# One phase for the final norm, the modulation and the norm rows; turning and splitting inside the projection

## The chip, the cores and the metric

The program runs on one core of one Trainium2 chip. It is one launch; the metric is the device time of that launch in microseconds, from the first to the last instruction and what lies around them. The core has a matrix engine (TensorE, PE in the profile, its weight loads PEld), three elementwise engines (VectorE or DVE, ScalarE or ACT, GpSimd or POOL), a SyncE queue (SP) that only issues transfers here, and 16 DMA engines. Everything is float32; large products are made from operands split into two float32r parts (hi and lo, three products each).

## What is computed

Two layers of a first block, its final norm, and then a second block that takes the normed rows as `x`. The part around the change, cut from the reference:

```python
x = rms_norm(x, final_g)                              # end of the first block, x: 512 x 1024
mod_x = jnp.split(jax.nn.silu(c) @ w_mod + b_mod, 6)  # second block; w_mod: 1024 x 6144
mod_c = ...                                           # the same for c_ctx
zx = modulate(rmsnorm(x, norm1_g), mod_x[0], mod_x[1]) @ w_in
zc = modulate(rmsnorm(ctx, norm1_g), mod_c[0], mod_c[1]) @ w_in   # ctx: 256 x 1024
...
x = x + mod_x[2] * merge_branches(...)
x = x + mod_x[5] * peer_ffn(modulate(rmsnorm(x, norm2_g), mod_x[3], mod_x[4]), ...)
```

`modulate(h, shift, scale)` is `h * (1 + scale) + shift`. So of the six 1024-wide parts of the modulation, four (0, 1, 3, 4) are needed as columns (one number per channel) and two (2, 5), the gates, as rows spread over all partitions.

## The kernel before

The kernel is a chain of phases. Each `Phase` allocates semaphores, opens a block in which every engine has its own list of instructions, and ends with a barrier of all engines. Within an engine the list runs in the order written; between engines only semaphores set the order. Rows of tokens lie in tiles of 128 (`ST` = 4 for x, `CT` = 2 for the context, `AT` = 6 for both), the 1024 channels in `DC` = 8 chunks of 128.

Between the last product of the first block and the first one of the second, these phases run one after the other:

- `load_phase` for `final_g` (`fg`), then `norm_phase` with `write_back`: ScalarE sums the squares of four row tiles, VectorE scales each tile in place (L213).
- `modulation_phases`: a `load_phase` of six small transfers, a phase for the silu (`csil`) and a copy of it spread 128 wide (`cwide`), then `plain_gemm_phase` over the twelve blocks of `w_mod` (each 1024 x 512, 2048 KB, ring `wbuf_mod` of four, loaded by SyncE at L356). For eight blocks TensorE multiplies `csil` (2 columns) by the block, eight chunks into one bank of `psum` (L367), and VectorE copies two rows out (L1251). For the four gate blocks it multiplies `cwide`, so that the sum comes out on all 128 partitions, and VectorE adds the bias rows (L1258). A last phase turns the pairs into columns with small products (L1274) and VectorE makes `affine` from them.
- `load_phase` of the context rows, then `norm_phase` through `modulated_norm` twice, for 2 and for 4 tiles: squares, root, scaled rows (L210), transposes (L226), modulation out of `psum` into `hT_whole` (L1299).
- `split_phase`: ScalarE writes `hT_all.hi` (L578), VectorE `hT_all.lo` (L584), SyncE spills `x` and `hT_whole` to HBM (L563) and loads the rope tables and gains (L569).
- `gemm_phase`, the projection: six blocks of `w_in_2`, each loaded in four quarters of 512 KB through `w_raw` (a ring of 2 here), cast to hi by ScalarE (L521), lo by VectorE (L534), and multiplied (L472). A quarter's lo frees its place in the ring. `HeadNorm` is its side: an object whose methods are called at given places of each engine's list; `lead_vector` builds tables before the first quarter, and later it norms and rotates rows of q and k while the next groups are multiplied. In the fifth and sixth block, groups of transposes (`Turns`, L458) stand between the groups of products.

A second `gemm_phase`, in the last stage of the kernel, already has a norm as its side: `ModulatedLead` makes norm rows, transposes them ahead of the first product, and modulates and splits two chunks between every two weight quarters (L318, L312, L322). A third one, after the attention, has `MixerSpill` as its side, whose transfers are issued by GpSimd while the first weights load.

## Time and profile before

| | |
|---|---|
| median of 3 runs | 5360.02 us (5355.99 to 5365.32) |
| profiled execution | 5353.26 us, span 5351.4 us |
| TensorE busy | 4554.2 us, 85% of the span |
| VectorE busy | 3130.4 us, 58% |
| ScalarE, GpSimd busy | 1602.2 us, 739.5 us |
| mean granted TensorE clock | 0.933 of full speed |

The page also cuts the span into 40 equal slices of 134 us and gives each engine's busy share in tenths. TensorE stands at 7 to 9 in nearly all of them; slices 13 and 14 (1605 to 1873 us), in which the phases listed above lie, are both at 7. The share is an average over stages that have little to do with each other, so a question on one stage is put to the timeline of that stage: the instructions of each engine in order of time, with the idle time before each and what ended it. Times there are microseconds from the start of the span.

### The profile page before, as it was taken

Reading aid. Unit: us, or ns where it says so; the run is one execution under the profiler, and the core shown is the slowest. Engines: PE = TensorE matmul, PEld = TensorE weight load, DVE = VectorE, ACT = ScalarE, POOL = GpSimd, SP = SyncE. Lnnn points to the kernel's source line nnn. Section 1 sums busy time; section 2 is a strip of 40 time slices with the busy share of each in tenths; the row PEclk is TensorE's granted clock in tenths of the full one; section 3 lists DMA queues with packets and bytes.
Section 4 is the critical chain, followed back from the end, with each engine's and each line's share of the span. In section 5 each row is a group of like instructions: output and inputs, shape, how many; then the busy total and the mean of one; then the engine's idle time right before and its main releaser. Section 6 shows DMA issues by size and latency. Waiting matters only on the chain. (4 is left out here: it accounts for less than half of the span.)

```text
span 5351.4 us, 57195 instructions
## 1 busy us (share of the span) xinstructions
PE 4554.2 (85%) x20624; PEld 3197.2 (60%) x20624; DVE 3130.4 (58%) x6299; ACT 1602.2 (30%) x3154; POOL 739.5 (14%) x650
## 2 busy tenths in 40 slices
PE   7878998978997597788999999997986877777777
PEld 5636886735884285566888888886862333333333
DVE  5563224563221265755777777753438888888886
ACT  3233342233341133312544444543221111111111
POOL 0000010000110000010000000000004444444443
PEclk9978998978998799988999999998998999999998
DMA  3002332101334320041000000004229999999998
GB/s 117 32 0 79 102 98 75 48 1 63 100 98 159 128 75 2 1 151 63 10 12 12 12 12 12 12 3 142 89 71 382 419 412 416 414 410 413 410 413 346
DMA packets 142504, 777.72 MB, mean 145 GB/s; under 512 B 18932, under 2 KB 23924, under 8 KB 74120
## 3 DMA queue, kind: packets, MB, share of 16 engines
q0 software_dynamic: 78576, 557.79, 25.5%
q1 hardware_dynamic: 63640, 216.19, 12.1%
q8 instruction: 169, 2.77, 0.2%
q14 instruction: 119, 0.97, 0.1%
HBM read 753.99 MB, written 19.92 MB: 145 GB/s over the span
## 5 line engine op out<-in xcount | busy, mean ns | idle before, releaser
L2730 PE MATMUL psum<-rows,diag 128*128 128x512 f32 x2048 | 999.0, 645 | 317.7 <-ACT diag L2709 313.2
L2730 PEld LDWEIGHTS psum<-rows,diag 128*128 128x128 f32 x2048 | 411.1, 206 | 887.8 <-issue 887.8
L534 DVE TENSOR_TENSOR w_split_lo<-w_raw,w_split_hi 128x1024 fp32r<-128x1024 f32 (+1 forms) x316 | 379.4, 1209 | 649.2 <-ACT w_split_hi L521 644.4
L2620 POOL DMA_INDIRECT rows<-in_peer_uv,sel_idx x512 | 614.9, 1201 | 935.4 <-PE psum L2730 648.3
L2635 DVE SCALAR_TENSOR_TENSOR uh<-rows,h_rows 128x1024 f32<-128x1024 f32 x512 | 627.8, 1226 | 181.6 <-DMA rows<-in_peer_uv,sel_idx 153.3
L521 ACT CAST w_split_hi<-w_raw 128x1024 fp32r<-128x1024 f32 (+1 forms) x316 | 322.8, 1028 | 788.5 <-PE psum L472 465.7
L2702 ACT ACTIVATE g<-g 128x4 f32<-128x4 f32 x128 | 26.3, 205 | 1077.0 <-DVE g L2646 1077.0
L740 POOL TENSOR_TENSOR uT_lo<-normed_rows,uT_hi 128x512 fp32r<-128x512 f32 x64 | 82.8, 1294 | 1378.9 <-ACT uT_hi L716 1378.9
L1812 PE MATMUL psum<-X_wide,wAT_wide 128*128 128x128 f32 x1920 | 262.2, 280 | 1.1 <-DVE X_wide L2156 1.1
L1812 PEld LDWEIGHTS psum<-X_wide,wAT_wide 128*128 128x128 f32 x1920 | 234.8, 192 | 34.3 <-issue 31.2
L1823 PE MATMUL psum<-U_wide,Y_wide 128*128 128x128 f32 x1536 | 206.0, 277 | 0.0
L472 PE MATMUL psum<-hT_mlp_hi,w_split_hi 128*128 128x512 f32 x512 | 199.6, 390 | 2.2 <-DVE hT_mlp_lo L287 2.2
L1823 PEld LDWEIGHTS psum<-U_wide,Y_wide 128*128 128x128 f32 x1536 | 188.0, 192 | 19.0 <-issue 18.7
L472 PE MATMUL psum<-hT_mlp_hi,w_split_lo 128*128 128x512 f32 x512 | 199.2, 389 | 0.0
L472 PE MATMUL psum<-hT_mlp_lo,w_split_hi 128*128 128x512 f32 x512 | 199.2, 389 | 0.0
L472 PE MATMUL psum<-w_split_hi,uT_hi 128*128 128x512 f32 x512 | 199.2, 389 | 0.0
L472 PE MATMUL psum<-w_split_lo,uT_hi 128*128 128x512 f32 x512 | 199.2, 389 | 0.0
L472 PE MATMUL psum<-w_split_hi,uT_lo 128*128 128x512 f32 x512 | 199.2, 389 | 0.0
L1993 ACT COPY U_wide<-psum 128x512 f32<-128x512 f32 x240 | 140.6, 586 | 187.5 <-PE psum L1812 184.0
L2124 DVE SCALAR_TENSOR_TENSOR wS<-psum,pl,wP 128x128 f32<-128x128 f32 x160 | 54.8, 343 | 204.7 <-PE psum L1888 204.7
L2709 ACT ACTIVATE diag<-ident_sb,g 128x128 f32<-128x128 f32 x512 | 163.5, 390 | 36.6 <-DVE g L2651 36.6
L2353 POOL DMA_DIRECT2D merge_stage<-hT_spill x8 | 4.3, 538 | 1178.9 <-POOLq L168 1170.9
(471 smaller groups left out, 9299.7 us busy)
## 6 DMA issues: line engine op xcount, KB each, us to landing
w_raw<-in_w_in SPq DMA_DIRECT2D x120, 512.0 KB, 4.7
w_raw<-in_w_up SPq DMA_DIRECT2D x64, 512.0 KB, 4.3
w_raw<-in_w_down SPq DMA_DIRECT2D x64, 512.0 KB, 4.4
wbuf_mod<-in_w_mod SPq DMA_DIRECT2D x12, 2048.0 KB, 7.5
w_raw<-in_w_out SPq DMA_DIRECT2D x24, 512.0 KB, 5.1
w_raw<-in_peer_wq SPq DMA_DIRECT2D x16, 512.0 KB, 4.8
rows<-in_peer_uv,sel_idx POOLq DMA_INDIRECT x512, 13.2
w_raw<-in_w_branch_a SPq DMA_DIRECT2D x8, 512.0 KB, 4.5
```

The costliest lines, as they stand in the source:

```text
L472: last = nc.tensor.matmul(psum[0:rows, bank, 0:cols], l_, r_, start=(start and c == 0 and j == 0), stop=(stop and c == len(pairs) - 1 and ...
L521: nc.scalar.copy(ring.hi[:, q % SPLIT_RING, :, 0:w], raw[:, q % raw_ring, :, 0:w]).then_inc(hi_ready, 1)
L534: nc.vector.tensor_tensor(ring.lo[:, q % SPLIT_RING, :, 0:w], raw[:, q % raw_ring, :, 0:w], ring.hi[:, q % SPLIT_RING, :, 0:w].bitcast(F32 ...
L740: return nc.gpsimd.tensor_tensor(uT.lo[:, k, :], squares[:, k % 2, :], uT.hi[:, k, :].bitcast(F32), ALU.subtract)
L1812: last = nc.tensor.matmul(psum[:, b, i * P:(i + 1) * P], flat(wAT[:, c]), flat(X[:, c]), start=True, stop=True)
L1823: last = nc.tensor.matmul(psum[:, b, i * P:(i + 1) * P], l_, r_, start=True, stop=True)
L1993: nc.scalar.copy(flat4(U[:, batch(b)]), psum[:, b, :]).then_inc(u_copied, 1)
L2124: nc.vector.scalar_tensor_tensor(wS[:], psum[:, 5, 0:P], scale, wP[:], ALU.mult, ALU.add).then_inc(s_copied, 1)
L2620: nc.gpsimd.indirect_dma_start(out=rows[:, n % RB, :], out_offset=None, in_=I["peer_uv"], in_offset=bass.IndirectOffsetOnAxis(ap=sel[:, t, ...
L2635: nc.vector.scalar_tensor_tensor(prod[:], rows[:, n % RB, 0:D], 1.0, h[:, t, :], ALU.mult, ALU.mult, accum_out=dots[:, (n // BATCH) % 2, s ...
L2709: nc.scalar.activation(diag[:, n % (2 * BATCH), :], ident[:], ACT.Copy, scale=g2[:, b % 2, i:i + 1]).then_inc(diag_ready, 1)
L2730: last = nc.tensor.matmul(psum[:, 2 * (t % 2) + half, :], diag[:, n % (2 * BATCH), :], rows[:, n % RB, D + half * NB:D + (half + 1) * NB], ...
```

## The change

All phases before the projection become one, `modulation_phase`. In it:

- SyncE loads the condition vector and then the twelve blocks of `w_mod` in another order (pairs and gates in turn); the other small loads, the context rows and `final_g` are issued by GpSimd.
- ScalarE and VectorE make the final norm and, after it, the norm rows of context and x (`xn`, in what will be `v`), between the pieces of the modulation.
- The gates leave TensorE: VectorE multiplies and adds the eight chunks of a gate block with the silu as a scalar per partition (`sum_gate`), and TensorE spreads the sum over the partitions with one product by ones (`spread`).
- The columns are turned in two halves (`columns`).

The projection gets `ModulatedHeads` as its side, which adds to `HeadNorm` what `norm_phase` and `split_phase` did: transposes ahead of the first product, modulation and split of two chunks after each weight quarter, the context's transposes as four `Turns` in the first block, spills and table loads from GpSimd. The tables are built in the second block.

```diff
+def modulation_phase(nc, T, x, xn, sb):
...
+    BLOCKS = ((0, 0), (0, 1), (1, 0), (1, 1), (2, 0), (3, 0), (2, 1), (3, 1), (5, 0), (4, 0), (5, 1), (4, 1))
...
+        @block.sync
+        def _(sp):
+            sp.dma_start(csil[:], I["c"]).then_inc(cond_loaded, 16)
+            for b, (m, half) in enumerate(BLOCKS):
+                before = b - SLOTS4
+                if before in pairs:
+                    sp.wait_ge(pair_ready, pairs.index(before) + 1)
+                elif before in gates:
+                    sp.wait_ge(gate_summed, gates.index(before) + 1)
+                sp.dma_start(wbuf[:, b % SLOTS4], I["w_mod"][2 * m + half]).then_inc(block_loaded[b % SLOTS4], 16)
...
+            def sum_gate(i):
...
+                chain.after(nc.vector.tensor_scalar(a, wbuf[:, b % SLOTS4, 0, :], csil[:, 0, 0:1], None, ALU.mult))
+                for c in range(1, DC):
+                    ins = nc.vector.scalar_tensor_tensor(a, wbuf[:, b % SLOTS4, c, :], csil[:, c, 0:1], a, ALU.mult,
+                                                         ALU.add)
...
+            for i in range(4):
+                pair(i)
+            columns(0)
+            pair(4)
+            spread(0)
+            pair(5)
+            spread(1)
+            pair(6)
+            spread(2)
+            pair(7)
+            spread(3)
+            columns(1)
...
+class ModulatedHeads(HeadNorm):
...
+    def gpsimd(self, pool):
+        nc = self.nc
+        nc.gpsimd.dma_start(*self.x_to).then_inc(self.x_spilled, 16)
+        pool.wait_ge(self.x_spilled, 16)
+        for dst, src in self.table_loads:
+            nc.gpsimd.dma_start(dst, src).then_inc(self.tables_loaded, 16)
+        for c in range(DC):
+            pool.wait_ge(self.whole_ready, c + 1)
+            nc.gpsimd.dma_start(self.hT_to[:, c, :], self.whole[:, c, CTX:]).then_inc(self.hT_spilled, 16)
...
+    def quarter_scalar(self, act, chain, q):
+        for c in range(QC * q, QC * q + QC):
+            act.wait_ge(self.whole_ready, c + 1)
+            self.nc.scalar.copy(self.hT.hi[:, c, CTX:], self.whole[:, c, CTX:]).then_inc(self.hi_scaled, 1)
+
+    def quarter_vector(self, dve, chain, q):
+        for c in range(QC * q, QC * q + QC):
+            dve.wait_ge(self.transposed, c + 1)
+            self.modulate(self.whole[:, c, CTX:], self.psum[:, c, :], 0, c).then_inc(self.whole_ready, 1)
+        for c in range(QC * q, QC * q + QC):
+            dve.wait_ge(self.hi_scaled, c + 1)
+            self.nc.vector.tensor_tensor(self.hT.lo[:, c, CTX:], self.whole[:, c, CTX:],
+                                         self.hT.hi[:, c, CTX:].bitcast(F32), ALU.subtract
+                                         ).then_inc(self.operand_ready, 1)
+
+    def operand(self, pe, b, c):
+        if b == 0:
+            pe.wait_ge(self.operand_ready, c + 1)
+        if b == 2 and c == 0:
+            pe.wait_ge(self.ctx_ready, 4)
...
+        if (b, g) == (1, 3):
+            act.wait_ge(self.hT_spilled, 16 * DC)
+            act.wait_ge(self.ctx_ready, 4)
...
+        if (b, g) == (1, 1):
+            dve.wait_ge(self.tables_loaded, 16 * len(self.table_loads))
+            self.tables(dve)
+        if (b, g) == (1, 3):
+            dve.wait_ge(self.hT_spilled, 16 * DC)
```

TensorE's list from the modulation to the first product of the projection: before, with `wbuf_mod` the blocks, `cwide` and `csil` the silu, `nscr` the norm rows:

```order
L367 MATMUL psum<-wbuf_mod,csil 2x512 x32
L367 MATMUL psum<-wbuf_mod,cwide 128x512 x16
L367 MATMUL psum<-wbuf_mod,csil 2x512 x32
L367 MATMUL psum<-wbuf_mod,cwide 128x512 x16
...
L1274 MATMUL psum<-ident_sb,mod_rows 128x2 x32
...
L226 MATMUL psum<-ident_sb,nscr 128x128 x16
...
L226 MATMUL psum<-ident_sb,nscr 128x128 x32
```

The same stretch of TensorE's list now, in which the last row stands in the projection's own phase and `arena` holds the norm rows:

```order
L1253 MATMUL psum<-wbuf_mod,csil 2x512 x32
L1271 MATMUL psum<-ident_sb,mod_rows 128x2 x16
L1253 MATMUL psum<-wbuf_mod,csil 2x512 x8
L1263 MATMUL psum<-gate_sums,ones_all 128x512
...
L1253 MATMUL psum<-wbuf_mod,csil 2x512 x8
L1263 MATMUL psum<-gate_sums,ones_all 128x512
L1271 MATMUL psum<-ident_sb,mod_rows 128x2 x16
...
L1425 MATMUL psum<-ident_sb,arena 128x128 x32
```

The 32 products by `cwide` are gone and four by ones stand between the last four pairs; the small products are in two halves, one of them in the middle.

VectorE's list before, from the final norm (L213) through the modulation to the first norm rows (`nscr`) and `hT_whole`:

```order
L213 SCALAR_TENSOR_TENSOR x<-x,stats,fg 128x1024 x4
...
L1251 COPY mod_rows<-psum 2x512 x4
L1258 TENSOR_TENSOR gate_rows<-psum,gate_rows 128x512 x2
L1251 COPY mod_rows<-psum 2x512 x4
L1258 TENSOR_TENSOR gate_rows<-psum,gate_rows 128x512 x2
...
L210 TENSOR_SCALAR nscr<-x,stats 128x1024 x4
L1299 TENSOR_SCALAR hT_whole<-psum,affine 128x512 x8
```

VectorE's list now, from the final norm to the first gate sum, and then the start of the projection:

```order
L1165 SCALAR_TENSOR_TENSOR x<-x,final_stats,fg 128x1024 x4
L1182 COPY mod_rows<-psum 2x512
L1170 TENSOR_SCALAR norm_stats<-norm_stats 128x6
L1173 RECIPROCAL norm_stats<-norm_stats 128x6
...
L1182 COPY mod_rows<-psum 2x512
L1193 TENSOR_SCALAR gate_sums<-wbuf_mod,csil 128x512
L1195 SCALAR_TENSOR_TENSOR gate_sums<-wbuf_mod,csil,gate_sums 128x512 x7
L1182 COPY mod_rows<-psum 2x512 x2
...
L419 TENSOR_TENSOR w_split9_lo<-w_raw9,w_split9_hi 128x1024
L1430 TENSOR_SCALAR arena<-psum,affine 128x512 x2
L1444 TENSOR_TENSOR hT_all_lo<-arena,hT_all_hi 128x512 x2
```

The norm work stands among the copies of the pairs, each gate sum takes eight instructions, and the modulation and the split of x stand behind each weight quarter.

GpSimd's list, empty in this stretch before, now starts the projection with the spill of `x`, on which its table loads wait:

```order
L1414 DMA x_spill<-x 128x4096
L1417 DMA x<-in_ropeC 128x384
L1417 DMA x<-in_ropeS 128x384
L1417 DMA x<-in_q_gain 128x128
L1417 DMA x<-in_k_gain 128x128
L1420 DMA hT_spill<-arena 128x512 x8
```

Six transfers that SyncE issued ahead of the projection are now thirteen of GpSimd's during it.

## Rows read from the trace of the kernel before

**Rows 1.** Stages: us; busy (instructions) of PE, PEld, DVE, ACT, POOL; clock; DMA share; GB/s
```profile
1666.40:1863.70 197.30, 108.23 (x305) 42.50 (x305) 40.92 (x68) 23.55 (x39) 0.00 (x0) 0.74 0.44 171
1879.00:2045.00 166.00, 166.00 (x772) 138.24 (x771) 95.47 (x114) 48.89 (x70) 0.00 (x0) 1.00 0.17 55
```

**Rows 2.** SyncE's timeline: start, us, engine, line, operation, out<-in, count
```profile
1667.40 0.35 SPq L178 DMA_DIRECT2D fg<-in_final_g  x1
...
1694.55 68.12 SPq L356 DMA_DIRECT2D wbuf_mod<-in_w_mod  x12
1806.57 0.33 SPq L178 DMA_DIRECT2D ctx_rows<-in_ctx  x1
...
1857.34 94.95 SPq L441 DMA_DIRECT2D w_raw<-in_w_in  x20
```

**Rows 3.** TensorE's timeline, modulation, small products, first and fourth quarter of the projection
```profile
1701.94 9.89 PE L367 MATMUL psum<-wbuf_mod,csil 128*2 128x512 f32 x16 [36.24 <-DMA wbuf_mod<-in_w_mod]
1711.98 7.03 PE L367 MATMUL psum<-wbuf_mod,csil 128*2 128x512 f32 x16
1719.16 7.03 PE L367 MATMUL psum<-wbuf_mod,csil 128*2 128x512 f32 x16
...
1784.60 7.11 PE L367 MATMUL psum<-wbuf_mod,cwide 128*128 128x512 f32 x16 [0.30 <-PE psum L367]
1793.22 10.81 PE L1274 MATMUL psum<-ident_sb,mod_rows 2*128 2x2 f32 x64 [1.51 <-PEq L168]
...
1871.94 0.50 PE L472 MATMUL psum<-w_split_hi,hT_all_hi 128*128 128x512 f32 x1 [0.41 <-DVE w_split_lo L534]
```

**Rows 4.** Stages as in Rows 1: first weights landing; the small products
```profile
1702.00:1709.00 7.00, 7.00 (x10) 1.04 (x11) 0.00 (x0) 0.00 (x0) 0.00 (x0) 0.59 0.99 424
...
1791.70:1795.00 3.30, 1.79 (x18) 1.81 (x17) 0.69 (x1) 0.00 (x0) 0.00 (x0) 1.00 0.02 5
1795.00:1798.00 3.00, 3.00 (x23) 3.00 (x22) 0.00 (x0) 0.00 (x0) 0.00 (x0) 0.75 0.00 0
```

**Rows 5.** VectorE's groups: line, operation, out<-in, count | busy, mean ns | idle before
```profile
L815 DVE SCALAR_TENSOR_TENSOR av<-qkpad,taps,av 128x512 f32<-128x512 f32 x64 | 48.1, 752 | 2.3
L813 DVE TENSOR_SCALAR av<-qkpad,taps 128x512 f32<-128x512 f32 x16 | 7.6, 477 | 0.0
L1251 DVE COPY mod_rows<-psum 2x512 f32<-2x512 f32 x8 | 5.4, 679 | 63.8 <-PE psum L367 63.8
```

**Rows 6.** VectorE's timeline at the end of the modulation
```profile
1804.06 0.42 DVE L1286 TENSOR_TENSOR modc<-psum,bcol 128x32 f32<-128x32 f32 x2 [11.63 <-PE psum L1274]
...
1805.53 0.17 DVE L1291 COPY affine<-modc 128x8 f32<-128x8 f32 x1
```

**Rows 7.** Timelines of ScalarE and TensorE: first weight quarter of the projection; the phase with `ModulatedLead`
```profile
1861.33 1.04 ACT L521 CAST w_split_hi<-w_raw 128x1024 fp32r<-128x1024 f32 x1 [14.78 <-DMA w_raw<-in_w_in]
...
3896.33 1.03 ACT L521 CAST w_split_hi<-w_raw 128x1024 fp32r<-128x1024 f32 x1
...
3913.92 0.47 PE L472 MATMUL psum<-hT_ps_hi,w_split_hi 128*128 128x512 f32 x1 [1.40 <-DVE hT_ps_lo L322]
```

**Rows 8.** VectorE and ScalarE: third weight quarter, projection and the phase with `MixerSpill`
```profile
1862.41 2.46 DVE L534 TENSOR_TENSOR w_split_lo<-w_raw,w_split_hi 128x1024 fp32r<-128x1024 f32 x2 [3.06 <-ACT w_split_hi L521]
1867.52 1.05 ACT L521 CAST w_split_hi<-w_raw 128x1024 fp32r<-128x1024 f32 x1 [3.91 <-DMA w_raw<-in_w_in]
...
2291.15 2.52 DVE L534 TENSOR_TENSOR w_split_lo<-w_raw,w_split_hi 128x1024 fp32r<-128x1024 f32 x2 [10.85 <-ACT w_split_hi L521]
2300.95 1.04 ACT L521 CAST w_split_hi<-w_raw 128x1024 fp32r<-128x1024 f32 x1 [8.53 <-DMA w_raw<-in_w_in]
```

**Rows 9.** TensorE's timeline in the fifth block; GpSimd's timeline in the last projection
```profile
1982.24 1.04 PE L458 MATMUL psum<-ident_sb,q_rows 128*128 128x128 f32 x8
1983.03 0.47 PE L472 MATMUL psum<-w_split_hi,hT_all_hi 128*128 128x512 f32 x1
...
3656.76 2.13 POOL L2353 DMA_DIRECT2D merge_stage<-hT_spill  x4 [1170.93 <-POOLq L168]
```

More of the change, by code:

```diff
@@ L551, in _ @@
                         tail(n).then_inc(tail_done, 1)
-def split_phase(nc, src, dst, spill=None, source=None, also=()):
-    with Phase(nc, ["hi_ready", "spilled", "moved"] + [f"chunk_loaded{c}" for c in range(DC)]) as (
-            block, hi_ready, spilled, moved, *chunk_loaded):
-        @block.sync
-        def _(sp):
-            if spill is not None:
-                for to, what in spill:
-                    sp.dma_start(to, what).then_inc(spilled, 16)
-                sp.wait_ge(spilled, 16 * len(spill))
-            if source is not None:
-                for c in range(DC):
-                    sp.dma_start(src[:, c, :], source[:, c, :]).then_inc(chunk_loaded[c], 16)
-            for d_, s_ in also:
-                sp.dma_start(d_, s_).then_inc(moved, 16)
-            if also:
-                sp.wait_ge(moved, 16 * len(also))
-        @block.scalar
-        def _(act):
-            for c in range(DC):
-                if source is not None:
-                    act.wait_ge(chunk_loaded[c], 16)
-                nc.scalar.copy(dst.hi[:, c, :], src[:, c, :]).then_inc(hi_ready, 1)
-        @block.vector
-        def _(dve):
-            for c in range(DC):
-                dve.wait_ge(hi_ready, c + 1)
-                nc.vector.tensor_tensor(dst.lo[:, c, :], src[:, c, :], dst.hi[:, c, :].bitcast(F32), ALU.subtract)
 def hybrid_layer(nc, l, T):
@@ L1272, in _ @@
                     for c in range(DC):
                         at = 2 * (q * DC + c)
-                        last = nc.tensor.matmul(psum[:, 0, at:at + 2], mod_rows[:, q, c * P:(c + 1) * P],
-                                                T["ident"][0:2, 0:2], start=True, stop=True)
+                        last = nc.tensor.matmul(psum[:, 6 + h, at:at + 2], rows[:, 2 * h + q, c * P:(c + 1) * P],
+                                                ident[0:2, 0:2], start=True, stop=True)
                 last.then_inc(columns_ready, 1)
-            @block.vector
@@ L1336, in turned, with tables @@
         return src[:, t, half * NB:(half + 1) * NB]
-    def lead_vector(self, dve, chain):
+    def tables(self, dve):
         nc = self.nc
@@ L2804, in sba, with with_context, both @@
                 return att.enter_context(nc.sbuf_tensor(name, shape, dt))
-            share = Share(arena)
-            v, k = share.take([AT, D]), share.take([AT, D])
             q = sba("q_rows", [P, ST, D])
             with nc.sbuf_tensor("head_squares", [P, D], F32) as sq:
-                heads = HeadNorm(nc, T, q, k, room, sq, (ropes, gains))
+                whole = k.rearrange("p t n -> p (t n)").rearrange("p (c n) -> p c n", c=DC)
+                heads = ModulatedHeads(nc, T, q, k, room, sq, (ropes, gains), v, whole, hT, (x_d, x[:]), hT_d,
+                                       [(ropes[:, 0], I["ropeC"]), (ropes[:, 1], I["ropeS"]),
+                                        (gains[:, 0], I["q_gain"].to_broadcast([P, 2, 64])),
+                                        (gains[:, 1], I["k_gain"].to_broadcast([P, 2, 64]))])
+                def with_context(groups):
+                    def both(w):
+                        g = groups(w)
+                        r = [heads.ctx_turns(j) for j in range(4)]
+                        return [g[0], r[0], g[1], r[1], g[2], r[2], r[3], g[3]]
+                    return both
                 def with_turns(groups, order):
```

387 lines of the change are left out of this document (210 added, 177 removed).

## Prediction

> **What bounds the kernel now.** I began with the engines' busy shares and the 40 slices: TensorE leads, but an average says nothing of one stage. So I put the question to the stage that the change rewrites. From VectorE's last addition of the first block to the first product of the projection 197.3 us pass [rows 1]. In them TensorE is busy 108.2 us, VectorE 40.9, ScalarE 23.6 and the DMA engines 44% of the time: nothing is full. SyncE's timeline shows why. It is a row of starts, each behind a barrier: the final gain at 1667.4, the first modulation block at 1694.6, the context rows at 1806.6, the projection's weights at 1857.3 [rows 2]. The path that sets the end runs through all of it, since nothing else is in flight.
>
> Two stretches of it are work at a limit. The modulation's twelve blocks occupy TensorE from 1701.94 to 1784.60 + 7.11 = 1791.7, at 7.18 us a block once the clock is up (7.03 busy, the next starts 1719.16 − 1711.98 = 7.18 later); the first takes 9.89 because it begins at the lower clock [rows 3]. The mean granted clock of 1702 to 1709 is 0.59 of 2.4 GHz [rows 4]. The rest, some 107 us, is loads, norms, barriers and splits with TensorE mostly idle.
>
> Behind it, from 1879 to 2045, the projection keeps TensorE busy for all of 166.0 us at the full clock, with VectorE busy 95.5 us of them and ScalarE 48.9 [rows 1]. So what this stage gains arrives at the end of the kernel, unless the projection gives it back, and every TensorE instruction added to the projection is paid in full.
>
> **The new modulation phase, step by step.** Times continue the trace's own clock. I follow TensorE's list, since it is the longest one, and look at the others as cover.
>
> Start. SyncE's first issue stands at 1667.4 as before; the condition vector takes 0.4 us of its queue, so block 0 is issued at 1667.8. Before, issue to first product took 1701.94 − 1694.55 = 7.4 us [rows 2, 3], alone on the engines. Now GpSimd's loads run beside it. The final gain spread over 128 partitions is 0.52 MB, 1.2 us at the 424 GB/s that the first blocks reached [rows 4]. First product: 1667.8 + 7.4 + 1.2 = **1676.4**. With no sharing it is 1675.2; with the 1.05 MB of context also ahead it is 1678.9. The silu needs only the condition vector and stands behind two square sums on ScalarE, so it is ready while block 0 is still landing.
>
> Four pairs: 9.89 + 0.15 + 3 × 7.18 = 31.6, to 1708.0. VectorE's copy 0.7 [rows 5], then the first half of the small products. Before, 64 records took 10.8 us [rows 3], but not evenly: 18 − 1 + 23 = 40 had begun by 1798, 4.8 us after their start, and between 1795 and 1798 the mean clock was 0.75, after 1.0 until 1795 [rows 4]: it had fallen to its lower level. So 32 of them take about 4.0 us, to **1712.7**, and leave TensorE at the lower clock: small products let it fall. The next pair then costs as much as a first one, 9.89 instead of 7.03, or 2.9 more. It would cost nothing if the clock held through only 32 records; I keep it, since they end in the stretch with 0.75.
>
> Four pairs and three products by ones: 4 × 7.18 + 2.9 + 3 × 0.9 (a block's 16 records take 7.03, so one product is two records, 0.88) = 34.3, to 1747.0. The last product by ones 0.9 beside VectorE's copy, the second half of the small products 4.0, VectorE's last step 0.8 (half of the sequence from 1804.06 to 1805.70) [rows 6]: 1752.7. From VectorE's last instruction to SyncE's next issue 1806.57 − 1805.70 = 0.9 passed [rows 2, 6]. The projection's first load is issued at **1753.6**, not at 1857.3.
>
> Cover for this: the transfers. Twelve blocks are 25.2 MB, GpSimd's loads 2.6; at 424 GB/s that is 66 us, under the 76 that TensorE's list takes. But the ring of four ties loads to uses. Block 9 goes into the place of block 5, whose pair is ready at 1722.8, and lands some 7.4 later, at 1730.2, when TensorE is done with the pair before it at 1730.9 plus a product by ones: just hidden. Block 11 queues behind 9 and 10 and lands at about 1740, where TensorE arrives at 1740.0. These two have no slack; each us of delay there costs one.
>
> Cover by VectorE: a gate sum is 0.48 + 7 × 0.79 = 6.0 us (0.75 an instruction and a wait between them) [rows 5], four of them 24 us. The first needs block 4 (landed by 1702) and must be over when TensorE wants the copies of pairs 2 and 3, at 1708. By this sum it is over at 1708. Late blocks push it beyond, up to 4 us. The final norm and the norm rows, a handful of long instructions, lie in the waits for pairs 0 and 1, which leave VectorE nearly 30 us.
>
> **The lead of the projection.** It now has the shape of `ModulatedLead`. There, from the cast of the first quarter at 3896.33 to the first product of the fourth quarter at 3913.92, after which TensorE does not stop, 17.6 us pass [rows 7]. The first quarter's cast comes 1861.33 − 1857.34 = 4.0 us after the load's issue [rows 2, 7]. What differs is the spill of x, 2.1 MB on GpSimd's queue at the same moment. No row has just this. The nearest is the phase with `MixerSpill`: there the third quarter was cast 2300.95 − 2293.67 = 7.3 us after VectorE freed both places, against 1867.52 − 1864.87 = 2.7 in the quiet case, so 4.6 us of delay beside 3.6 MB of GpSimd's transfers [rows 8]. Bounds 0 and 4.6; I take 2.0, less than half, since here the spill is smaller and only the first quarter has no slack (each later one has about 2 us). Fourth quarter: 1753.6 + 4.0 + 2.0 + 17.6 = **1777.2**, where before it was 1871.94 [rows 3]. That is 94.7 us earlier.
>
> A rule of the Trainium skill ("DMA: Bandwidth & Descriptors", the section on SWDGE, HWDGE and iDMA) bears on the 2.0: an engine takes turns between the queues of the two kinds. If a weight packet waits for one of four times its size each time, the whole spill goes ahead of the first quarter, and the estimate by that would be near 5 us (2.1 MB at the measured 424 GB/s), a time of 5270. The delay in the rows on `MixerSpill` agrees in kind; no row here shows the turns themselves.
>
> **What the projection pays.** The context's 16 transposes: eight took 0.79 us at the full clock [rows 9], so 1.6. VectorE gains some 10 us of modulation, split and tables in the first two blocks, where it had room; TensorE has all eight banks ahead of it and no new wait before block 2. The waits for the spill stand at the last group of block 1, about 40 us after the lead.
>
> **Sum.** 94.7 − 1.6 = 93.1 us. The profiled execution took 5353.3 us; minus 93.1 it is 5260.2. The median of the runs is 6.8 us above the profiled one; the forecast is made against the median: 5360.0 − 93.1 = **5266.9**.
>
> **Rivals.**
> *The lead starves.* The weights get little of the engines beside the spill, and a second quarter loses its slack too: the whole 4.6 at the first, 4 more at the third as in [rows 8]. For it: a ring of 2, and 16 KB of a partition in a row in the spill. Against: SyncE issues first and GpSimd's issue itself takes 0.53 [rows 9]. Price 6 to 7: 5273.
> *The ring binds the modulation.* Blocks 8 to 11 are freed by gate sums and pairs in turn; if the first sum ends late (DMA shared with GpSimd's loads) or the clock falls again in a gap, a 2.9 for each fall and up to 4 for the sum, the phase ends 7 to 10 later: 5276.
> *Less than thought.* The clock holds through the small products (2.9 back), no contention in the lead (2.0), none at the start (1.2): 5261.
> *Slower than before.* The spill holds the projection. ScalarE and VectorE both stop at the last group of block 1 until all eight pieces of `hT_spill` have landed, behind them the splits of block 2's weights, behind those TensorE. The pieces are due by about 1822 (1777 plus seven groups of 5.5 and the transposes). GpSimd has 13 issues from 1754 on, 0.53 each when nothing holds it [rows 9], 7 us in all, done by 1785. It decides from 5 us an issue on, and to lose 93 us more than 12 us an issue would be needed (13 × 12.4 = 161 us after 1754): above 5371. Nothing in the trace is near it.
> On this the Trainium skill has a rule that speaks against the change ("SBUF — State Buffer", the box on DVE blocking DMA): a transfer issued by GpSimd is held while VectorE copies in its fast mode, with 620 ns becoming 3100 ns. By that page 13 issues would take 40 us, ending at 1794, and nothing would be late. The trace has 0.53 an issue with VectorE at work in the same stage.
>
> **How the numbers follow.** Forecast (5262 to 5271) 0.50; lead starves 0.14; ring binds 0.20; less than thought 0.13; slower than before 0.01; 0.02 for a gain under 0.2%, if the gain is given back by something I don't see. About 0.2%, 11 us, is what a measurement can tell from no change. The terms' own ends, −6 and +13, with the runs' spread of −4 and +5, not all at once, give **5256 to 5284**, which also holds the first three rivals. Faster by over 0.2%: 0.97, same 0.02, slower 0.01.
>
> **What would show it.** The first pair near 1676 at the lower clock, its last near 1747; the clock at 0.5 after the first small products; SyncE's first projection weights near 1754; TensorE without a gap from about 1777; no idle time of TensorE in blocks 0 to 3. I am wrong if TensorE waits for VectorE's gate sums or for blocks 9 and 11, if the first quarter's cast comes more than 8 us after its issue, or if a later stage changes its length.

## The result and the profile after

The changed kernel took 5263.32 us (median of 4 runs, 5259.79 to 5289.91), the kernel before beside it 5358.86 us (4 runs, 5355.99 to 5365.32). The ratio is 0.9827, with a 95% interval of 0.981 to 0.9844: faster by 95.5 us. The forecast was 5266.9 us in a range of 5256 to 5284.

The profiled execution took 5262.22 us. Engines over the whole span, from its page:

```profile
span 5260.4 us, 56898 instructions
PE 4544.4 (86%) x20568; PEld 3189.7 (61%) x20568; DVE 3151.8 (60%) x6333; ACT 1603.0 (30%) x3153; POOL 753.5 (14%) x671
```

TensorE's work has fallen by 9.8 us only; the other 81 of the 91 us between the two spans are waits. SyncE's timeline (start, us, engine, line, operation, out<-in, count) has one start where [rows 2] have four:

```profile
1666.09 0.35 SPq L1107 DMA_DIRECT2D csil<-in_c  x1
1666.49 63.60 SPq L1114 DMA_DIRECT2D wbuf_mod<-in_w_mod  x12
1752.52 138.10 SPq L326 DMA_DIRECT2D w_raw<-in_w_in  x24
1958.38 0.33 SPq L178 DMA_DIRECT2D lam_rows<-in_diff_lambda  x1
```

The phase begins at 1666.09, where `fg` was issued at 1667.40 before [rows 2], so 1.3 us are scatter of what lies ahead. I count from this first issue. The projection's weights are issued 86.4 us after it (before 189.9), and `lam_rows`, the first load after the projection, 292.3 us after it. Before, `lam_rows` was issued at 2052.90, 385.5 us after the start. The stage has become **93.2 us** shorter; the sum said 93.1. Of the kernel before there is one traced execution only, so its 385.5 us carry the scatter of one.

TensorE's timeline, with the idle time before in brackets, is to be read beside [rows 3]:

```profile
1674.97 29.65 PE L1253 MATMUL psum<-wbuf_mod,csil 128*2 128x512 f32 x64 [10.59 <-DMA wbuf_mod<-in_w_mod]
1707.74 5.14 PE L1271 MATMUL psum<-ident_sb,mod_rows 2*128 2x2 f32 x32 [3.12 <-DVE mod_rows L1182]
1712.81 8.91 PE L1253 MATMUL psum<-wbuf_mod,csil 128*2 128x512 f32 x16
1721.65 1.13 PE L1263 MATMUL psum<-gate_sums,ones_all 128*128 128x512 f32 x2
...
1739.19 7.03 PE L1253 MATMUL psum<-wbuf_mod,csil 128*2 128x512 f32 x16 [0.38 <-DMA wbuf_mod<-in_w_mod]
1746.14 1.12 PE L1263 MATMUL psum<-gate_sums,ones_all 128*128 128x512 f32 x2
1747.20 3.77 PE L1271 MATMUL psum<-ident_sb,mod_rows 2*128 2x2 f32 x32
...
1775.77 0.47 PE L357 MATMUL psum<-w_split_hi,hT_all_hi 128*128 128x512 f32 x1 [1.41 <-DVE hT_all_lo L1444]
```

Two waits are worth reading. The 3.12 us ahead of the first small products are VectorE's: its timeline shows the copies of pairs 2 and 3 behind the whole first gate sum, although the products of both pairs were over by 1704.6.

```profile
1678.44 4.87 DVE L1165 SCALAR_TENSOR_TENSOR x<-x,final_stats,fg 128x1024 f32<-128x1024 f32 x4 [6.93 <-DMA fg<-in_final_g]
...
1700.50 0.49 DVE L1193 TENSOR_SCALAR gate_sums<-wbuf_mod,csil 128x512 f32<-128x512 f32 x1 [5.07 <-DMA wbuf_mod<-in_w_mod]
1701.03 5.48 DVE L1195 SCALAR_TENSOR_TENSOR gate_sums<-wbuf_mod,csil,gate_sums 128x512 f32<-128x512 f32 x7
1706.42 1.27 DVE L1182 COPY mod_rows<-psum 2x512 f32<-2x512 f32 x2
```

The other is in the projection's lead. Its first weight quarter is cast 4.85 us after its issue, and the third waits 0.85 us for its load (ScalarE's timeline):

```profile
1757.37 1.05 ACT L406 CAST w_split_hi<-w_raw 128x1024 fp32r<-128x1024 f32 x1 [61.38 <-DMA w_raw<-in_w_in]
...
1766.92 1.04 ACT L406 CAST w_split_hi<-w_raw 128x1024 fp32r<-128x1024 f32 x1 [0.85 <-DMA w_raw<-in_w_in]
```

while GpSimd's queue moves the spill of x, whose 2.1 MB take 13 us:

```profile
1752.99 0.54 POOL L1414 DMA_DIRECT2D x_spill<-x  x1 [82.23 <-POOLq L168]
1766.57 0.55 POOL L1417 DMA_DIRECT2D x<-in_ropeC  x1 [13.04 <-DMA x_spill<-x]
```

Stretches (us; busy of PE, PEld, DVE, ACT, POOL; clock; DMA share; GB/s): the projection as in the second of [rows 1], and the small products with the pair behind them, as in [rows 4]:

```profile
1780.00:1946.00 166.00, 166.00 (x772) 138.17 (x771) 104.23 (x130) 51.52 (x74) 0.00 (x0) 1.00 0.18 57
1707.00:1710.00 3.00, 2.26 (x20) 2.26 (x20) 0.69 (x2) 0.00 (x0) 0.00 (x0) 0.97 1.02 437
1710.00:1713.00 3.00, 3.00 (x15) 2.88 (x16) 0.08 (x1) 0.00 (x0) 0.00 (x0) 0.50 1.01 431
1713.00:1720.00 7.00, 7.00 (x13) 1.19 (x12) 6.34 (x13) 0.00 (x0) 0.00 (x0) 0.74 0.82 346
```

The projection has taken in VectorE's extra work (104.2 us busy where it had 95.5) and still holds TensorE busy for all of the 166 us.

All of TensorE's waits between the phase's start and the end of the projection fit in four rows (waited for: us in total, times, longest):

```profile
PE psum L1253 <- DMA wbuf_mod<-in_w_mod: 11.0, 2, 10.6
PE psum L357 <- DVE hT_all_lo L1444: 8.4, 4, 3.2
PE psum L1271 <- DVE mod_rows L1182: 3.1, 1, 3.1
PE psum L1425 <- PEq L168: 1.6, 1, 1.6
```

### The profile page after: what moved, and what is told of

It reads as the page before. It is cut to its first block and busy times, and to the rows that moved or that the text cites. A ratio compares the mean times of both kernels' runs of the same rounds, so it can differ in the third digit from the quotient of the medians.

```text
span 5260.4 us, 56898 instructions
## 1 busy us (share of the span) xinstructions
PE 4544.4 (86%) x20568; PEld 3189.7 (61%) x20568; DVE 3151.8 (60%) x6333; ACT 1603.0 (30%) x3153; POOL 753.5 (14%) x671
## 5 line engine op out<-in xcount | busy, mean ns | idle before, releaser
L2809 PE MATMUL psum<-rows,diag 128*128 128x512 f32 x2048 | 1019.7, 656 | 296.5 <-ACT diag L2788 295.1
L2714 DVE SCALAR_TENSOR_TENSOR uh<-rows,h_rows 128x1024 f32<-128x1024 f32 x512 | 628.0, 1227 | 181.0 <-DMA rows<-in_peer_uv,sel_idx 152.0
```

The source lines that it names most:

```text
L2714: nc.vector.scalar_tensor_tensor(prod[:], rows[:, n % RB, 0:D], 1.0, h[:, t, :], ALU.mult, ALU.mult, accum_out=dots[:, (n // BATCH) % 2, s ...
L2809: last = nc.tensor.matmul(psum[:, 2 * (t % 2) + half, :], diag[:, n % (2 * BATCH), :], rows[:, n % RB, D + half * NB:D + (half + 1) * NB], ...
```

## The experiments

A run's median moves by some microseconds, more than most of the terms in question. So each kernel has two readings: its time, and from its trace the distance from the phase's first issue to the first product of the projection's fourth quarter (Q4) and to the load of `lam_rows`. The last column, from there to the end of the span, is code whose work no experiment changes (the kernels with weights loaded ahead give a later phase's weight ring another place).

| | time, us (runs) | to Q4 | to `lam_rows` | rest |
|---|---|---|---|---|
| before | 5357.7 to 5363.1 (its medians beside the rows below) | 204.5 | 385.5 | 3298.5 |
| changed kernel | 5263.3 (4) | 109.7 | 292.3 | 3302.0 |
| the same again | 5264.0 (4) | 109.8 | 292.4 | 3302.2 |
| the same again | 5265.3 (5) | 109.1 | 291.7 | 3301.2 |
| modulation phase alone | 5287.4 (4) | 131.8 | 312.5 | 3304.7 |
| projection's part alone | 5339.3 (10) | 183.6 | 367.8 | 3321.9 |
| gates on TensorE | 5286.7 (4) | 129.1 | 313.2 | 3298.1 |
| first columns late | 5270.3 (4) | 113.1 | 295.7 | 3302.1 |
| first gate sum later | 5266.8 (4) | 107.9 | 292.4 | 3299.2 |
| spill of x later | 5263.8 (4) | 107.9 | 292.1 | 3303.0 |
| two quarters ahead | 5261.3 (4) | 105.4 | 289.5 | 3301.7 |
| two of the three | 5261.4 (5) | 104.0 | 288.2 | 3306.2 |
| all three | 5273.8 (5) | 103.0 | 285.6 | 3319.1 |
| all three again | 5259.4 (5) | 102.4 | 286.4 | 3308.1 |

**The changed kernel again**, to see how far two measurements of it differ.

> The changed kernel once more, as the reference for the others of its call. Both theories: 5263 us, a ratio of 0.982 to the kernel before, the first product of the projection's fourth weight quarter about 109.7 us after SyncE's first issue of the modulation phase.

5263.95 us, ratio 0.9816 (0.9785 to 0.9846). The wait ahead of the small products was there again, 3.24 us, so it is no accident of one execution.

**Each part alone.** First the merged phase, with turning, split and tables in phases of their own ahead of the projection:

```diff
+        turn_phase(nc, T, v, CT, 0, 1, whole, 0)
+        turn_phase(nc, T, v, ST, CT, 0, whole, CTX)
+        split_phase(nc, whole, hT, spill=[(x_d, x[:]), (hT_d, whole[:, :, CTX:])], also=[...])
...
-                heads = ModulatedHeads(nc, T, q, k, room, sq, ...)
+                heads = TableHeads(nc, T, q, k, room, sq, (ropes, gains))
...
-                gemm_phase(nc, psum, [(W[0], with_context(rows_of(q, 0, CT, ST))), ...
+                gemm_phase(nc, psum, [(W[0], rows_of(q, 0, CT, ST)), ...
```

> One part alone: the merged modulation phase stays, but the turning, the modulation, the split and the spills stand in phases of their own ahead of the projection, as before the change. Theory (the two parts are separate rows of starts, their gains add): the phases put back cost about 5.0 + 0.9 for the context, 7.7 + 0.7 for x and 16.8 for the split and spills, less 8.7 that the projection's own start is shorter (14.6 instead of 23.3 from the first load to the fourth quarter), less 1.6 of context transposes: about 21 us more than the changed kernel, 5284. Rival (most of the gain comes from what runs inside the projection): 45 us more or beyond, 5308.

5287.35 us, ratio 0.9859 (0.9828 to 0.989). Then the reverse: final norm, modulation and norm rows in their old phases, and `ModulatedHeads` in the projection.

```diff
-            modulation_phase(nc, T, x, v, ...)
+            modulation_phases(nc, T, wbuf)
...
+            load_phase(nc, [(ctx_rows[:], I["ctx"])])
+            norm_phase(nc, psum, ident, ctx_rows, CT, (scr, v[:, 0:CT]), T["stats"], None)
+            norm_phase(nc, psum, ident, x, ST, (scr, v[:, CT:AT]), T["stats"], None)
```

> The other part alone: final norm, modulation (gates on TensorE) and the norm rows in their old separate phases, but turning, modulation and split of the rows inside the projection, as changed. Theory (gains add): what mod_only lacks, so about 19 to 21 us less than the kernel before, 5339, with some 76 us kept from the merged phase alone. Rival (most of the gain is in the projection): 45 us less, 5314.

5339.32 us, ratio 0.9961 (0.9946 to 0.9976). By the traces the merged phase is worth 385.5 − 312.5 = 73.0 us, the projection's part 17.7, together 90.7 of the 93.2. The gains add but for 2.5 us. A part of these is the clock and not the two edits: from Q4 to `lam_rows` the trace of the projection's part took 184.2 us, the changed kernel 182.6 (more on this below). At Q4 the merged phase is worth 204.5 − 131.8 = 72.7 us, the projection's part 20.9, together 93.6 of 94.9. Where the last 1.3 us arise wasn't separated.

**The gates back on TensorE**, all else as changed:

```diff
-            def spread(i):
-                pe.wait_ge(gate_summed, i + 1)
...
-                nc.tensor.matmul(psum[:, 4 + i % 2, :], ones[:], acc[:, i % 2, :], start=True, stop=True
-                                 ).then_inc(gate_spread, 1)
+            def gate(i):
...
+                for c in range(DC):
+                    last = nc.tensor.matmul(psum[:, 4 + i % 2, :], cwide[:, c, :], wbuf[:, b % SLOTS4, c, :],
+                                            start=(c == 0), stop=(c == DC - 1))
```

> The changed kernel with the gates back on TensorE, inside the merged phase: four blocks of 7.18 us are multiplied by the silu spread 128 wide, VectorE's gate sums and the four products by ones are gone. Theory (TensorE's list sets the length of the phase): 4 x 7.18 - 4 x 1.06 - 2.4 (the copies of pairs no longer wait behind a gate sum) = 22 us more, 5285, and TensorE without waits for weights after the first block. Rival (the ring of loads sets it already): at most 10 us more, 5273.

5286.7 us, ratio 0.987 (0.9835 to 0.9905). By the traces Q4 came 19.4 us later and `lam_rows` 20.9; the 1.5 between them is again the clock behind Q4 (184.1 us for 182.6). Its timeline of TensorE has a gate block at 7.1 us, and the second small products with a wait of 0.77:

```profile
1759.17 7.13 PE L1249 MATMUL psum<-wbuf_mod,cwide 128*128 128x512 f32 x16
1766.24 7.03 PE L1237 MATMUL psum<-wbuf_mod,csil 128*2 128x512 f32 x16
1774.04 3.73 PE L1258 MATMUL psum<-ident_sb,mod_rows 2*128 2x2 f32 x32 [0.77 <-DVE mod_rows L1181]
```

So TensorE's list did bind the phase, and 19 to 21 of the 93 us are gates that left it; 22 were expected. The rival, by which the loads would have bound it after half of that, fell.

**The first columns at the end.** Both halves of the small products stand behind the last pair:

```diff
@@ vector and tensor @@
-            columns(0)
...
+            columns(0)
             columns(1)
```

> The changed kernel with the first half of the small products (the columns of parts 0 and 1) moved from the middle of TensorE's list to its end, ahead of the second half. Theory 1 (TensorE's list alone sets the phase; small products in the middle cost a wait for VectorE, 3.1 us, and a slower pair, 1.9): those 5.0 go, the two halves in a row take 10.8 instead of 5.1 + 3.8 as the clock falls in them: 3 us less than the changed kernel, 5260. Theory 2 (behind it the loads bind: blocks land one per 5 us and 9 and 11 are freed by pairs): TensorE waits for blocks 7, 9 and 11, the last pair still ends near 1742.6, and the end of the phase comes 3 to 4 us later than now, 5267.

5270.29 us, ratio 0.9825 (0.9796 to 0.9855), and Q4 came 3.4 us later. TensorE's timeline has three waits for loads where the changed kernel had one of 0.38 us, and the pair behind the longest of them ran at a lower clock (last row, stretch as above):

```profile
1707.04 7.03 PE L1253 MATMUL psum<-wbuf_mod,csil 128*2 128x512 f32 x16 [0.97 <-DMA wbuf_mod<-in_w_mod]
...
1716.73 7.03 PE L1253 MATMUL psum<-wbuf_mod,csil 128*2 128x512 f32 x16 [1.60 <-DMA wbuf_mod<-in_w_mod]
...
1727.43 8.72 PE L1253 MATMUL psum<-wbuf_mod,csil 128*2 128x512 f32 x16 [2.61 <-DMA wbuf_mod<-in_w_mod]
```

```profile
1727.40:1730.40 3.00, 2.97 (x5) 0.56 (x6) 2.89 (x5) 0.00 (x0) 0.00 (x0) 0.64 0.94 404
```

The second theory holds: the small products in the middle fill time in which the ring's loads land, and moving them behind the last pair buys nothing.

**The first gate sum behind the copies.** The direct test of the step that my sum had too short:

```diff
-            sum_gate(0)
             take_pair(2)
             take_pair(3)
+            sum_gate(0)
```

> VectorE copies pairs 2 and 3 before it takes the first gate sum, not after it. Theory (the 3.1 us that TensorE waits ahead of the first small products are the gate sum that stands in VectorE's list before the copies): the wait shrinks to 0.7, the phase ends 2.4 us earlier, 5261. Rival (the loads take the place: block 8 is freed by that gate sum, later now): the wait goes and comes back ahead of a later pair, 0 us.

5266.76 us, ratio 0.9827 (0.9796 to 0.9859): no gain in the time. The trace shows that the cause was right. VectorE copies pair 3 first, and TensorE waits 0.77 instead of 3.12 us (VectorE's, then TensorE's timeline):

```profile
1706.77 0.68 DVE L1182 COPY mod_rows<-psum 2x512 f32<-2x512 f32 x1 [6.19 <-PE psum L1253]
1707.38 0.47 DVE L1193 TENSOR_SCALAR gate_sums<-wbuf_mod,csil 128x512 f32<-128x512 f32 x1
```

```profile
1707.50 3.73 PE L1271 MATMUL psum<-ident_sb,mod_rows 2*128 2x2 f32 x32 [0.77 <-DVE mod_rows L1182]
...
1729.92 7.03 PE L1253 MATMUL psum<-wbuf_mod,csil 128*2 128x512 f32 x16 [0.97 <-DMA wbuf_mod<-in_w_mod]
...
1739.62 7.03 PE L1253 MATMUL psum<-wbuf_mod,csil 128*2 128x512 f32 x16 [1.61 <-DMA wbuf_mod<-in_w_mod]
```

The shorter wait also spares the small products: they ran at the full clock, which fell only behind them, in the next pair (8.72 us).

```profile
1707.00:1710.00 3.00, 2.50 (x23) 2.50 (x23) 2.89 (x5) 0.00 (x0) 0.00 (x0) 1.00 0.97 415
...
1713.00:1716.00 3.00, 3.00 (x6) 0.56 (x5) 2.82 (x9) 0.00 (x0) 0.00 (x0) 0.62 1.01 426
```

And the trace shows where the gain went. Of 2.35 us less wait and 1.4 less in the small products (3.73 for 5.14), 2.2 were lost again at once to loads (0.97 and 1.61, where 0.38 stood). 1.8 us were left at Q4, and at `lam_rows` nothing. Between these two the clock stood otherwise. With this edit alone Q4 stands at 1775.98, and the stretches around it read

```profile
1773.00:1776.00 3.00, 1.60 (x5) 0.72 (x4) 2.97 (x5) 1.24 (x2) 1.06 (x2) 0.50 1.00 395
1776.00:1779.00 3.00, 3.00 (x8) 2.32 (x9) 1.79 (x2) 1.04 (x1) 0.01 (x1) 0.50 0.95 351
1779.00:1782.00 3.00, 3.00 (x14) 2.55 (x13) 0.77 (x1) 1.05 (x1) 0.00 (x0) 0.81 0.73 238
```

In the changed kernel, with Q4 at 1775.77, they read

```profile
1772.80:1775.80 3.00, 1.59 (x5) 0.71 (x3) 2.97 (x5) 1.30 (x3) 1.07 (x2) 0.69 1.02 389
1775.80:1778.80 3.00, 3.00 (x15) 2.46 (x16) 1.77 (x2) 0.99 (x1) 0.01 (x1) 1.00 1.01 385
```

In the changed kernel the granted clock rose in the 3 us ahead of Q4. With the edit it rose 3 us or so after Q4, and 8 products stand where 15 did. Over the 12 traces that have Q4 in this form the distance from Q4 to `lam_rows` takes two values, 182.6 us in five and 184.0 to 184.5 in seven. In the five the clock was 1.00 from Q4 on. In five of the seven it stood at 0.50 or 0.51 for the first 3 us behind Q4, and in two (spill later, two of the three) it was 1.00 at Q4, fell within 1.5 us and came back some 3 us later. An edit alone doesn't decide it: one and the same kernel, with all three edits, took 182.6 us in one trace and 184.0 in the other.

**The spill of x behind the last modulated chunk**, so that it doesn't run beside the first weight quarters:

```diff
     def gpsimd(self, pool):
         nc = self.nc
+        pool.wait_ge(self.whole_ready, DC)
         nc.gpsimd.dma_start(*self.x_to).then_inc(self.x_spilled, 16)
```

> GpSimd issues the spill of x only when all eight chunks of the modulated rows are written, not at the start of the projection. Theory (the spill takes the DMA engines from the weight quarters: the first is cast 4.85 us after its issue instead of 4.0, the third waits 0.95): both go, the fourth quarter's product starts 1.8 us earlier, 5261.5. Rival (the lead's pace is VectorE's and ScalarE's): 0 to 0.5 us.

5263.76 us, ratio 0.9823 (0.979 to 0.9856). The issue stood at 1753.06, and ScalarE's timeline reads

```profile
1756.89 1.04 ACT L406 CAST w_split_hi<-w_raw 128x1024 fp32r<-128x1024 f32 x1 [60.27 <-DMA w_raw<-in_w_in]
...
1765.48 1.04 ACT L406 CAST w_split_hi<-w_raw 128x1024 fp32r<-128x1024 f32 x1
```

3.83 us from issue to cast instead of 4.85, and no wait at the third quarter: against that trace the spill cost 1.0 and 0.85 us. The other two traces of the changed kernel have 4.78 and 4.75 us to the first cast, and a wait of 0.38 at the third or 0.59 at the second quarter. So the spill cost 0.9 to 1.0 us at the first quarter and 0.4 to 0.9 at one later. Q4 came 1.8 us earlier, and as above nearly all of it, 1.6, was gone at `lam_rows`, with the clock at 0.64 and 0.79 in the two stretches of 3 us behind Q4.

**The first two quarters ahead of the projection.** SyncE loads them behind the last modulation block, into a place that both later users of a ring of two share:

```diff
+            for q in range(2):
+                sp.dma_start(raw[:, q], I["w_in_2"][0][:, q * QC:(q + 1) * QC, :]).then_inc(ahead_loaded, 16)
+            sp.wait_ge(ahead_loaded, 32)
...
-                    act.wait_ge(raw_loaded[q % raw_ring], 16 * (q // raw_ring + 1))
+                    times = q // raw_ring + (ahead is None)
+                    if times:
+                        act.wait_ge(raw_loaded[q % raw_ring], 16 * times)
```

> The first two weight quarters of the projection are loaded at the end of the modulation phase, behind its last block, into a ring kept for them. Theory (the projection's start waits for its first weights and for nothing else): the first cast stands at the phase's start instead of 4.85 us later, 4.8 us less, 5258. Rival (the transposes and the barrier hold it): 2 us less or none.

5261.34 us, ratio 0.9812 (0.9783 to 0.9841). The first cast starts with its phase, the third waits for its load (ScalarE's timeline):

```profile
1750.91 1.05 ACT L412 CAST w_split_hi<-w_raw_first 128x1024 fp32r<-128x1024 f32 x1 [56.49 <-PEq L168]
...
1761.20 1.04 ACT L412 CAST w_split_hi<-w_raw_first 128x1024 fp32r<-128x1024 f32 x1 [1.60 <-DMA w_raw_first<-in_w_in]
```

Q4 came 4.3 us earlier, `lam_rows` 2.8: of an expected 4.8 a part.

**All three edits**, with the changed kernel beside them.

> The changed kernel with the three edits at once: the first gate sum behind the copies of pairs 2 and 3, the spill of x behind the last split of the rows, and the first two quarters of the projection's weights loaded at the end of the modulation's own loads. Taken one at a time they moved the first product of the fourth quarter, counted from the phase's first issue on SyncE, from 109.7 us to 107.9, 107.9 and 105.4. Theory 1 (three separate waits, the gains add): 109.7 - 1.8 - 1.8 - 4.3 = 101.8 us, and a time of 5263.3 - 7.9 = 5255.4 us. Theory 2 (the spill only cost by its share of the DMA engines while the first two quarters were on their way, and once these are loaded ahead moving it gives nothing): 103.6 us and 5257.2 us. Theory 3 (with the gate sum out of the way the loads of W_mod bind, and the two quarters queued behind them come too late for the first cast): the first cast waits for its DMA, 105 us or more, and 5259 us or more.

> The changed kernel once more, beside the one with the three edits and on the same chip, so that the two can be set against each other. By both theories of where the time went it is 5263.3 us again, within 2 us, with 109.7 us from the phase's first issue to the first product of the fourth quarter, and 3.1 to 3.2 us of wait ahead of the first small products. What can differ from run to run is the time of the stages behind: the step from the 2nd to the 3rd load of zk_tile was 120.34 us before, and 122.75 and 121.85 us in two runs of the changed kernel, but 120.74, 120.79 and 120.31 in three variants of it that differ only in the phase far ahead. Theory 1 (it is scatter of the run and no cost of the change): it falls between 120.3 and 122.8 again, at no fixed value. Theory 2 (a cost of the changed kernel): 121.8 or more.

The three edits gave 5273.78 us (5254.7 to 5282.13), ratio 0.9823 (0.9799 to 0.9848); the changed kernel 5265.33 (5261.74 to 5279.11), ratio 0.9825 (0.9805 to 0.9844). In the trace the edits did what they should: Q4 103.0 us after the start, between the first two theories, and `lam_rows` 6.1 us earlier. In the last unit of the scan stage, where both kernels run the same code, that trace has this clock:

```profile
3505.00:3525.00 20.00, 16.78 (x69) 11.95 (x68) 2.44 (x6) 4.66 (x17) 0.00 (x0) 0.70 0.00 1
3525.00:3545.00 20.00, 18.80 (x64) 13.18 (x63) 2.08 (x5) 3.16 (x12) 0.00 (x0) 0.50 0.00 1
3545.00:3565.00 20.00, 15.91 (x51) 10.30 (x52) 3.46 (x6) 2.09 (x8) 0.00 (x0) 0.50 0.00 0
```

and SyncE's three spills of the stage take 208.23 us; the changed kernel's, on its timeline, 190.08:

```profile
3370.78 190.08 SPq L1838 DMA_DIRECT2D obT_spill<-x  x3
```

That is 18.2 us, three times what the edits gained. The trace of the projection's part alone has the same step at 206.34 us, with a clock of 0.50, and none of the edits.

The third theory of the same text also fails: loads bind a little more (0.41 and 1.68 us of wait), but the first cast waits for nothing. For theory 2 on the changed kernel, the step from the second to the third load of `zk_tile` took 120.75 us this time: scatter, no cost of the change.

**Two edits, and all three again.** To see whether the spill still counts once the quarters lie ready, and whether the edits bring the fall of the clock.

> The changed kernel with two of the three edits: the first two quarters of the projection's weights loaded ahead, and the spill of x behind the last split of the rows. The first gate sum stands where it does in the changed kernel. With all three edits the first product of the fourth quarter came 103.0 us after the phase's first issue, with the weights alone 105.4. Theory 1 (gains of separate waits add): 105.4 - 1.8 = 103.6 us, and a time near 5257. Theory 2 (the spill cost nothing any more, once the two quarters lay ready): 105.4 us, and a time near 5259.

> The kernel with the three edits once more. In its profiled execution (5273.78 us) it was 6 us ahead of the changed kernel after the projection, as its edits say, and lost 18 us in the last part of the scan stage, 3505 to 3575 us, where the granted clock fell to 0.50; the steps of SyncE around it took 208.2 us where 189.9 to 191.5 us stand in other executions, and 206.3 us in one execution of the kernel with the projection's part alone, which does not have the edits. Theory 1 (the clock falls there in some executions of every kernel and has nothing to do with the edits): executions fall in two groups again, near 5255 to 5258 and near 5273 to 5282, the first holding most of them. Theory 2 (the edits bring it on): most executions near 5273 to 5282 again, more than of the kernel with two edits beside it.

5261.4 us (5258.54 to 5266.06), ratio 0.9807 (0.9789 to 0.9825), for two; 5259.35 (5257.01 to 5262.98), ratio 0.9802 (0.9784 to 0.9821), for all three. Q4 stood at 104.0 with two: the spill still counts, 1.4 of its 1.8 us. No execution of the three edits lay above 5263 this time. So the long executions don't come with the edits each time, and single ones of that kind stand among the changed kernel's too (5279.11, 5289.91); what makes the clock fall there was not found. The median of all ten executions with the three edits is 5259.6 us, that of all 13 of the changed kernel 5264.1. These 4.5 us agree with the 6 us in the traces, but are under the 0.2% that a measurement can tell. The version with three edits beats the kernel before, and the changed one by the stage's trace, but not by a time that shows it.

## Why the prediction was right, and where its steps were off

**The bound.** It said that this stage is a row of starts behind barriers, and that what it gains arrives at the end. The stage gave 93.2, 93.1 and 93.8 us in three traces of the changed kernel, for 93.1 predicted, and TensorE had no gap in the projection from Q4 on. That the mechanism held is shown; that the sum agrees to 0.1 us is in part luck. Counted from the first issue, Q4 was forecast at 109.8 us and came at 109.7, but the terms between were off by up to 1.2 us each: the start of the small products +0.4, the first small products +1.1, the pairs and products by ones −0.8, the end of the phase −0.4, issue to first cast −1.2, first cast to Q4 +0.8. Of the signs of being wrong that the text had named, three came, all small: a wait behind a gate sum (3.1 us), a wait for block 11 (0.38), and later stages that took 3.5 us more.

**The start.** 9.0 us from the phase's first issue to the first product were predicted, 8.9 measured. GpSimd's loads were slower than I had assumed. `fg` held VectorE until 1678.44, 11.9 us after its issue at 1666.59, but the final norm had room.

**Four pairs.** 31.6 predicted, 29.7 measured: the clock came up sooner, with a mean of 0.71 in the first 7 us where [rows 4] have 0.59.

**The first gate sum: the step that was too simple.** The text said the sum would be over when TensorE wants the copies of pairs 2 and 3, and gave the wait 0.7. The wait was 3.1. The sum ended 40.4 us after the start, where 40.6 was forecast, but two things stood beside it: TensorE was done with its pairs 2 us sooner, and both copies (1.27), not one, came behind the sum. The two errors nearly cancel, 2.4 more wait against 2.0 less work, and the small products began 41.6 us after the start for 41.3 forecast. This one isn't luck, by the timeline: VectorE waited for block 4 until 1700.50 before it began the sum, so a faster TensorE only waits longer there. With the sum moved the wait was 0.77.

**Small products.** 4.0 and 4.0 predicted, 5.1 and 3.8 measured, and 8.9 instead of 9.9 for the pair behind them. The fall of the clock was right in kind: 0.97 in the first 3 us, 0.50 in the next. But it came within the first small products and not only behind them, and the wait ahead goes with that: in the four traces where it was 0.77 us they took 3.73, in those where it was 3.0 to 3.2 us 4.95 to 5.39.

**The ring.** Block 11 cost 0.38 us, where the text gave 0. As it said, there was no slack: two edits that let TensorE run ahead, the later gate sum and the later columns, met the loads at once, with 2.6 and 5.2 us of wait for them. The rival *the ring binds the modulation* named both of these waits, at 7 to 10 us in all, and fell by their size; *less than thought* fell since the clock did drop and the loads did share.

**The lead.** 2.0 predicted for the spill, all of it at the first quarter; moving the spill showed 4.85 − 3.83 = 1.0 there and 0.85 at the third, where the text had seen 2 us of room. The interval from first cast to Q4 was 18.4 instead of 17.6, and that 0.85 is the difference. The rival *the lead starves* named the same mechanism with 6 to 7 us and fell. The estimate by the Trainium skill ("DMA: Bandwidth & Descriptors", the section on SWDGE, HWDGE and iDMA) was near 5 us for the first quarter: the queues do share, as the 1.0 us shows, but the spill doesn't go ahead whole; it landed 9 us after that cast.

**The price in the projection.** 1.6 predicted. From Q4 to `lam_rows` it was 182.6 us against 2052.90 − 1871.94 = 181.0 before: 1.6. That holds for the three traces of the changed kernel, in all of which the clock was at 1.00 from Q4 on.

**The slower rival.** It needed over 5 us for each of GpSimd's issues; they took 0.54 (the rows above). The rule of the Trainium skill that speaks for it ("SBUF — State Buffer", the box on DVE blocking DMA) is about copies of VectorE in its fast mode, and no run here tests it: at the spill's issue VectorE was idle (1751.47 to 1758.45), and beside the later ones it subtracted two tensors or scaled out of `psum`. The row that the prediction held against the rule doesn't test it either: in the trace before, VectorE was idle from 3652.98 to 3661.48, all through the four issues of [rows 9].

**The time itself.** By the trace: 1.3 us from the earlier start, 93.2 from the stage, and 3302.0 − 3298.5 = 3.5 given back behind it, 91.0 in all. That last term is within scatter, and its cause stays open: in 14 traces the rest took 3298.1 to 3308.1 us but for the two with the fallen clock, and the kernel before has just one of them, at the lower end. The gates on TensorE ran the same code there in 3298.1, so nothing in the changed kernel forces the 3.5. The median came out 3.6 us below the forecast: I had carried over the 6.8 us by which before's median lay above its profiled execution, where after's lay 1.1 above, and 2 us of trace went the other way.

## What to carry to other kernels

Where a stage is a chain of loads, barriers and half-idle engines, write down the one engine whose list becomes the longest once everything is merged, and sum that list; here it gave 93.1 for 93.2 us, with single terms off by up to 1.2. Then look at each point where a short copy that the long list waits for stands behind a long job on another engine, and put the copy first; and expect that a repair of one wait uncovers the next one, a load or a clock that comes up later, a couple of microseconds behind. With edits worth less than the scatter of a run, read the stage in the trace: the medians alone would not have told most of these variants apart.

## What the runs showed of the hardware

- After a wait of 3.1 us, the granted clock went from 0.97 (1707 to 1710 us) to 0.50 (1710 to 1713) in 32 products of two columns, and the pair behind them took 8.9 instead of 7.0 us. With a wait of 0.77 us it stayed at 1.00 in these products and was 0.62 in the pair behind (8.7 us). With no small products there, but a wait of 2.6 us, it was 0.64 in the pair behind (8.7 us too). So small products aren't the only thing that such a fall followed; a wait of a few us was another.
- Whether the clock stood at 1.00 or at 0.50 in the first microseconds of a long stream of products was worth 1.5 us (182.6 against 184.0 to 184.5), which took back gains of 1.8 us that edits had made just before; one kernel showed both in two executions.
- In two of 14 traces the clock fell to 0.50 for some 40 us and more in the last unit of the scan, and the step of SyncE around it took 206.3 and 208.2 us for 189.9 to 191.6 in eleven others, in kernels with and without the edits; the last had 195.6.
- A transfer of 2.1 MB by GpSimd beside SyncE's weight quarters cost the first of these 0.9 to 1.0 us and a later one 0.4 to 0.9, and took 13 us itself; moved away from them it took some 9.7.
